# Hybrid encoder layer: earlier attention-to-memory transposes, a held weight load in the MLP loop, and rows added in DRAM at the end

## What is computed

```python
h = rmsnorm(x, g_mix_pre)
q, k, v, u, qx, gates = split(h @ w_in)              # 512, 128, 128, 512, 512, 3 * 1024 columns
y_attn = sliding_window_attention(rope(q), rope(k), v, sinks)
y_ssm  = s5_branch(u, ...)                           # state space, GELU, GLU
y_mem  = memory_cross_attention(qx, km, vm)          # 4 heads, softmax over 256 memory tokens, then @ vm
merged = sum over branches of sigmoid(gate) * (y @ w_branch)
x = x + rmsnorm(merged @ w_out, g_mix_post)          # called x1 below
h = rmsnorm(x, g_mlp_pre)
f = square(relu(h @ w_up)) @ w_down                  # 4096 hidden columns
out = x + rmsnorm(f, g_mlp_post)
```

## Time and profile before

| what | value |
|---|---|
| median of three executions | 1457.79 us |
| the profiled execution, its own time | 1457.39 us |
| its span in the profile | 1455.5 us |
| PE busy | 1438.8 us (99%) |
| DVE busy | 1046.4 us (72%) |
| ACT busy | 524.3 us (36%) |
| POOL busy | 179.6 us (12%) |
| granted TensorE clock | 0.998 of full speed |
| DMA | 209.23 MB, 144 GB/s over the span |

### The profile page before, as it was taken

One profiled execution on the slowest core, in us unless ns is written; L12 is line 12 of the kernel. 1 busy time (PEld: TensorE's weight loads), 2 busy tenths in 40 slices (PEclk: granted clock), 3 DMA queues, 4 the chain that ended last, 5 costly groups with the idle time before them and its releaser, 6 DMA issues. The chain is left out here.

```text
span 1455.5 us, 18397 instructions
## 1 busy us (share of the span) xinstructions
PE 1438.8 (99%) x7046; PEld 1197.9 (82%) x7046; DVE 1046.4 (72%) x1723; ACT 524.3 (36%) x663; POOL 179.6 (12%) x287
## 2 busy tenths in 40 slices
PE   8999999999999999999999999999999999999997
PEld 7888888878888888888898888888888888888885
DVE  6768668647745734446756769697979697979878
ACT  4435853321221352311333532333433343424332
POOL 0000010030000021100100212301110202011110
PEclk9999999999999999999999999999999999999999
DMA  9301121542133187324333446946373727464545
GB/s 333 73 29 58 58 88 58 173 138 93 57 104 119 47 230 290 116 87 160 130 131 87 131 145 204 302 123 209 115 231 105 239 88 220 126 196 143 165 160 188
DMA packets 130322, 209.23 MB, mean 144 GB/s; under 512 B 21480, under 2 KB 72720, under 8 KB 130256
## 3 DMA queue, kind: packets, MB, share of 16 engines
q0 software_dynamic: 46176, 118.26, 25.6%
q1 hardware_dynamic: 84064, 90.07, 18.8%
q10 hardware_dynamic: 16, 0.00, 0.0%
HBM read 168.19 MB, written 40.11 MB: 143 GB/s over the span
## 5 line engine op out<-in xcount | busy, mean ns | idle before, releaser
L2083 PE MATMUL bank<-hThi,whi 128*128 128x512 f32 x800 | 314.0, 392 | 0.1
L2083 PE MATMUL bank<-hThi,wlo 128*128 128x512 f32 x800 | 311.5, 389 | 0.0
L2083 PE MATMUL bank<-hTlo,whi 128*128 128x512 f32 x800 | 311.4, 389 | 0.0
L2083 PEld LDWEIGHTS bank<-hThi,whi 128*128 128x128 f32 x800 | 150.2, 188 | 32.3 <-issue 1.2
L2083 PEld LDWEIGHTS bank<-hThi,wlo 128*128 128x128 f32 x800 | 150.2, 188 | 31.6
L2083 PEld LDWEIGHTS bank<-hTlo,whi 128*128 128x128 f32 x800 | 150.3, 188 | 30.6
L1162 ACT ACTIVATE whi<-raw 128x1024 fp32r<-128x1024 f32 x91 | 95.3, 1055 | 183.4 <-DVE raw L1887 96.8
L1877 DVE TENSOR_TENSOR wlo<-raw,whi 128x1024 fp32r<-128x1024 f32 x91 | 110.9, 1218 | 33.9 <-ACT whi L1162 33.9
L2483 PE MATMUL bank<-hThi,whi 128*128 128x512 f32 x336 | 130.8, 389 | 0.6 <-DMA hTlo<-h_scratch 0.6
L2503 PE MATMUL bank<-whi,yhi 128*128 128x512 f32 x336 | 130.8, 389 | 0.0
L2483 PE MATMUL bank<-hTlo,whi 128*128 128x512 f32 x336 | 130.7, 389 | 0.0
(11 more groups left out here) (398 smaller groups left out, 2563.3 us busy)
## 6 DMA issues: line engine op xcount, KB each, us to landing
hThi<-h_scratch POOLq DMA_DIRECT2D x42, 512.0 KB, 5.6
hTlo<-h_scratch POOLq DMA_DIRECT2D x42, 512.0 KB, 6.5
raw<-in_w_in_dram SPq DMA_DIRECT2D x34, 512.0 KB, 5.4
raw<-in_w_up_dram SPq DMA_DIRECT2D x32, 512.0 KB, 4.4
raw<-in_w_down_dram SPq DMA_DIRECT2D x32, 512.0 KB, 4.5
gate_scratch<-scr POOLq DMA_DIRECT2D x48, 256.0 KB, 2.6
tok<-gate_scratch POOLq DMA_DIRECT2D x24, 512.0 KB, 3.9
yhi<-h_scratch POOLq DMA_DIRECT2D x14, 512.0 KB, 5.8
```

The lines of the kernel that those rows point to most:

```text
L2083: ins = T.matmul(dst, lhs(k)[p], rhs(k)[q], start=start and k == 0 and i == 0, stop=stop and k == kt - 1 and i == 2)
```

## The change

It has three parts.

1. Memory attention: PE's transposes for q = 0 move ahead of the last of the four key/value pieces; ACT's `p_hi_of(0)` moves ahead of `turn(6)` and `turn(7)`; DVE's low parts for q = 0 move ahead of `rope(6)`.
2. The MLP loop: in iteration 0 SP waits for all of S_T3 (`third_in`) before it loads the down-projection weights.
3. The end: `x1` of six of the eight tiles is written straight into `out`, and of two into a smaller `x1_dram`. The inverse roots go to `mx` (DVE, `root`), ACT multiplies six tiles' rows by them in place (128x1024, in `yst` and in `raw`), and POOL adds them to `out` with an accumulating transfer. For the seventh tile ACT scales and POOL itself adds `x1` (`tensor_tensor`), and SP sends it. The eighth tile is finished by DVE as before.

```diff
+ROOTS = [(0, 1), (2, 3), (4, 5), (6,)]
+ROOT_AFTER = {4: 0, 7: 1, 11: 2, 13: 3}
+SCALE_AFTER = {5: (0, 1), 8: (2, 3), 12: (4, 5), 13: (6,)}
...
@@ SP, mlp(m, last)
+                if m == 0:
+                    for landed in third_in:
+                        sp.wait_ge(landed, 32)
                 unit_load(UP0, units[0], w_count(5, m))
                 unit_load(UP1, units[1], w_count(6, m))
...
@@ SP, the end
-            for t in range(NT):
-                sp.wait_ge(out_made, t + 1)
-                if t < NT - 1:
-                    sp.dma_start(rows[tile_of(t)], tok[:, (1 + t % 3) * D:(2 + t % 3) * D]).then_inc(out_sent[t % 3], 16)
...
+            sp.wait_ge(tile_added, 1)
+            sp.dma_start(out_rows[tile_of(NT - 2)], tok[:, 2 * D:3 * D]).then_inc(out_sent, 16)
+            for h in range(2):
+                sp.wait_ge(out_made, h + 1)
+                sp.dma_start(out_rows[tile_of(NT - 1), :, h * 512:h * 512 + 512], tok[:, D + h * 512:D + h * 512 + 512]).then_inc(out_sent, 16)
+            sp.wait_ge(out_sent, 48)
+            for s, count in enumerate((1, 1, 4)):
+                sp.wait_ge(out_added[s], 16 * count)
...
@@ POOL, x1 and the end
-                g.dma_start(x1_dram[t * P:(t + 1) * P, :], yx[:, t % 2, :]).then_inc(x1_sent, 16)
+                g.dma_start(x1_dram[t - tile_of(NT - 2)] if tile_of(t) > 5 else out_rows[t], yx[:, t % 2, :]).then_inc(x1_sent, 16)
...
-            for t in range(3, NT):
-                pool.wait_ge(out_sent[t % 3], 16 * (t // 3))
-                x1_load(t)
+            for t in range(NT - 2):
+                pool.wait_ge(rows_scaled, t + 1)
+                g.dma_start(out_rows[tile_of(t)], last_rows(t), accum_op=add).then_inc(out_added[min(t, 2)], 16)
+            pool.wait_ge(x1_back, 32)
+            pool.wait_ge(rows_scaled, NT - 1)
+            g.tensor_tensor(tok[:, 2 * D:3 * D], last_rows(NT - 2), tok[:, 2 * D:3 * D], add).then_inc(tile_added, 1)
...
@@ ACT, memory attention
-            for k in range(4, 8):
+            for k in range(4, 6):
                 turn(k)
...
             p_hi_of(0)
+            for k in range(6, 8):
+                turn(k)
...
@@ ACT, the end, after the square of piece i
+                for done in SCALE_AFTER.get(i, ()):
+                    k = done // 2
+                    act.wait_ge(root_made, k + 1)
+                    A.activation(last_rows(done), last_rows(done), ACT.Copy, scale=roots(k)[2][:, done % 2:done % 2 + 1]).then_inc(rows_scaled, 1)
...
@@ DVE, memory attention
             for i in range(2, 7):
+                if i == 6:
+                    p_low_of(0)
                 rope(i)
...
@@ DVE, the end
-                for k, t in enumerate(tiles):
-                    xt = tok[:, (1 + t % 3) * D:(2 + t % 3) * D]
-                    dve.wait_ge(x1_back[t % 3], 16 * (t // 3 + 1))
-                    for h in ([slice(0, D)] if t < NT - 1 else [slice(0, 512), slice(512, D)]):
-                        V.scalar_tensor_tensor(out=xt[:, h], in0=yx[:, t % 2, h], scalar=y[:, k:k + 1], in1=xt[:, h], op0=mul, op1=add)\
-                            .then_inc(out_made, 1)
...
+                if t > 5 and s == 0:
+                    dve.wait_ge(out_added[t - 6], 16)
+                mark(V.scalar_tensor_tensor(out=last_rows(t)[:, h], in0=a[:, h], scalar=float(D) ** 0.5, in1=tok[:, h], op0=mul, op1=mul))
+                if i in ROOT_AFTER:
+                    root(ROOTS[ROOT_AFTER[i]], roots(ROOT_AFTER[i]))
+                    dve.sem_inc(root_made, 1)
+            y7 = root((NT - 1,), [stat[:, k:k + 1] for k in range(4)])
+            dve.wait_ge(x1_back, 32)
+            for h in range(2):
+                c = slice(h * 512, h * 512 + 512)
+                V.scalar_tensor_tensor(out=tok[:, D + c.start:D + c.stop], in0=last_rows(NT - 1)[:, c], scalar=y7,
+                                       in1=tok[:, D + c.start:D + c.stop], op0=mul, op1=add).then_inc(out_made, 1)
...
@@ PE, memory attention
-            project(U_KV, FIRST["kv"])
-
+            project(U_KV, FIRST["kv"], range(3))
             pe.wait_ge(x_prob, 16)
...
             x_transposes(0)
+            project(U_KV, FIRST["kv"], range(3, 4))
```

More of the change, by code:

```diff
@@ L291, in hybrid_layer @@
         g_dram = nc.dram_tensor("gate_scratch", (3, KT, P, L), f32, kind="Internal").ap()
-        x1_dram = nc.dram_tensor("x1_scratch", (L, D), f32, kind="Internal").ap()
+        x1_dram = nc.dram_tensor("x1_scratch", (2, P, D), f32, kind="Internal").ap()
         u_dram = nc.dram_tensor("u_scratch", (4, P, L), f32, kind="Internal").ap()
@@ L348, in hybrid_layer @@
         step_made, step_hi, step_lo, step_out = sem("step_made"), sem("step_hi"), sem("step_lo"), [sem(f"step_out{k}") for k in range(2)]
-        x1_back = [sem(f"x1_back{s}") for s in range(3)]
-        out_made, out_sent = sem("out_made"), [sem(f"out_sent{s}") for s in range(3)]
+        root_made, rows_scaled = sem("root_made"), sem("rows_scaled")
+        x1_back, tile_added = sem("x1_back"), sem("tile_added")
+        out_made, out_added, out_sent = sem("out_made"), [sem(f"out_added{s}") for s in range(3)], sem("out_sent")
         chain = sem("chain")
@@ L481, in loaded, with roots, last_rows @@
             return w_loaded[slot], 16 * (2 * ((u - U_QX) // 2 + 1) + 2) + it * 64
+        def roots(k):
+            return [mx[:, 8 * k + 2 * j:8 * k + 2 * j + len(ROOTS[k])] for j in range(4)]
+        def last_rows(t):
+            return yst[:, 2 * (t % 2):2 * (t % 2) + 2, :].rearrange("p a c -> p (a c)") if t < 2 or t > 5 else \
+                raw[:, (t - 2) // 2, (t % 2) * D:(t % 2) * D + D]
+        out_rows = out[0].rearrange("(c i) d -> i c d", i=STEP)
         @block.sync
@@ L1479, in _, with p_low_of @@
             prep_lo(dve, U_KV + 1)
+            def p_low_of(q):
+                for m in range(2):
+                    n = FIRST["xpv"] + pv_event(q, m)
+                    dve.wait_ge(p_high, 2 * q + m + 1)
+                    V.tensor_tensor(p_low(q, m), banks[n % 8][:, :].rearrange("p (t c) -> p t c", t=4),
+                                    pT_hi[:, q % 2, m, :].rearrange("p (t c) -> p t c", t=4).bitcast(f32), sub).then_inc(bank_free[n % 8], 1)
             for i in range(2, 7):
+                if i == 6:
+                    p_low_of(0)
                 rope(i)
@@ L1486, in _ @@
                                   banks[n % 8][:, :].rearrange("p (j c) -> p j c", j=4)).then_inc(bank_free[n % 8], 1)
[L1488 to L1493, removed]
+            for q in range(1, 8):
+                p_low_of(q)
             rope(7)
@@ L2029, in _, with root @@
             up_phase(6, True)
-            def finish(tiles):
+            def root(tiles, places):
                 c, n = slice(tiles[0], tiles[-1] + 1), len(tiles)
-                v, nv, y, w = (stat[:, 2 * k:2 * k + n] for k in (0, 1, 2, 3)) if n == 1 else \
-                    (stat[:, 0:2], stat[:, 2:4], rs[:, 0:2], stat[:, 4:6])
+                v, nv, y, w = places
                 dve.wait_ge(sq_f, LAST_DOWN.index((tiles[-1], 1)) + 1)
@@ L2046, in finish @@
                     do(V.scalar_tensor_tensor(out=y, in0=w, scalar=1.5, in1=y, op0=add, op1=mul))
[L2047 to L2052 removed]
+                return y
             dve.wait_ge(last_gain, 16)
```

23 lines of the change are left out of this document (2 added, 21 removed).

## The result

The changed kernel takes 1460.59 us, the median of 13 runs (1459.08 to 1462.61); the kernel before takes 1457.77 on the same chips (13 runs, 1457.34 to 1458.89). The ratio is 1.0018, with a 95% interval of 1.0010 to 1.0025: 2.8 us slower. The forecast was 1456.9, with a range up to 1459.7, so the result lies outside it.

The account below looks back on a forecast made before the run. PE was taken as the bound, busy 1438.8 of 1455.5 us. Memory attention -1.0, hold +2.6 and end -2.5 summed to -0.9 us, giving a median of 1456.9 us, range 1453.9 to 1459.7.

Parts of the forecast that it names:

- Memory attention, -1.0: Memory attention: PE's 0.97 us wait before the first product with `vm` goes; 1.0 us less, ends 0.8 and 1.2.
- The hold, +2.6: MLP loop, iteration 0: down weights land at 939.6 instead of 936.9, delaying `w_diff` and dP3; 2.6 us more.
- ACT's copy of the first half: MLP loop: ACT's copy moves to about 935.6, its low part done before 938, so it doesn't come last.
- the landing term: MLP loop: the last down weights land at 939.6 in place of 936.9, 2.7 us later.
- The prediction's sign for this part: MLP loop, at dP3: PE would be seen waiting about 3 us for DVE's L1910 of before.
- The end, -2.5: After PE's last matmul: DVE keeps up, its last addition no longer 2.7 us late; less 0.2, 2.5 us less.
- I take no slowing: The end: POOL's addition beside DVE's last product costs DVE nothing; end of the estimate 1.5 us more.
- The rival with its mechanism: The end: POOL's addition blocks DVE, moving its last product and root by 1.0 us; 1457.9 us, chance 0.27.
- the last term: The sum's term for the end: 2.5 us less, or 1.0 by the skill's rule if POOL's addition takes 2.4.
- the 0.2 of the sum: The end: ACT's scalings delay the seventh tile's root and the last square by about 0.2 us, hence 2.7 - 0.2.
- The hold was not free: Rival, MLP loop: down weights still land by 937, dP3 starts as before; -3.6, 1454.2 us, chance 0.2.
- The accumulating transfers were not late: Rival, the end: accumulating transfers at four times a plain one land 3.0 us late; median 1459.9 us, chance 0.1.

Follow-up runs that it names:

- e1: Kernel before with only the memory-attention part (earlier transposes, high and low parts of q = 0): 1457.03 us against 1458.10, ratio 0.9994.
- e4: Changed kernel without the three lines of the hold: 1456.21 us, ratio 0.9983 to the kernel before.
- e3: Kernel before with only the new end: 1456.70 us, ratio 0.9989.
- e8: Kernel before with the hold, and DVE's `left_sum` put ahead of `w_lo_of(7)`: 1462.02 us, ratio 1.0028.
- e7: Kernel before, holding only the second two of the four down-weight transfers until S_T3 has landed: 1459.99 us, ratio 1.0015.
- e2: Kernel before with only the hold of the down-weight loads: 1463.46 us, ratio 1.0035.
- e6: e4 with POOL's addition replaced by a fill, so zeros are sent for the seventh tile: 1455.41 us against 1457.79 before, ratio 0.9982.
- e10: e4 with POOL's addition made to wait for DVE's last product: 1456.66 us, ratio 0.9994 to the kernel before.

## Why the prediction was wrong, step by step

**Memory attention, -1.0: right at its place and in the changed kernel.** -1.2 at the place, -1.07 by e1 (not told from nothing by its interval), and -0.5 as the difference of e4 and e3, where the rest is waited out in uP7. "A shift of PE's list ahead of the end is worth its full size" holds here only because the hold removed that pause.

**The hold, +2.6: wrong, and this decides the sign.** The landing of S_T3, the end of the pause in uP7, SP's issue and the equal shares of the queues came as forecast. That DVE's chain from `w_diff` decides when dP3 starts was right as well. Two steps that say when `w_diff` starts failed.

The first is a term that was put at nothing: "ACT's copy of the first half, released by its landing at 931.4, moves to about 935.6 and is done with its low part before 938, so it doesn't come last." The half landed at 937.74, and its low part was done at 940.1. Its two transfers took as long from issue to landing as before (7.4 and 9.5 us, before 7.5 and 9.9), so that with an issue 6.8 us later the half came 6.3 later, not 4.2. By 938 q1 had moved 1.9 MB, where the half is 1.05 MB, so the four transfers had been under way together. And I asked only whether the low part came before `w_diff`, the wait that I knew, and not what stood behind it in DVE's list. Behind it stood `left_sum`, whose banks PE wanted at 937.7. The two held `w_diff` back by 1.1 us beyond the last landing.

The second is the size of the landing term. It had 2.7 us; the landing was 3.9 later in e8 and, with PE's lead counted in, 4.1 in the changed kernel. The prediction let the first bytes move at about 930, and q1 moved its first in the microsecond from 931. This is why even e8 (4.2) stands above the 2.6, and e7, with two transfers held, near it (2.2). Together 1.4 + 1.1, and 0.1 that the prediction took off because PE would wait less at dP3 (it did not), are the 2.6 us by which the hold's 5.2 was missed.

The prediction's sign for this part, PE waiting about 3 us at dP3, did not show, though the mechanism was there: PE had already stood in uP4 and had only 0.3 us left to wait.

**The clock, not in the sum.** The prediction named no stretch at the lower clock, because PE had no wait over 1.0 us there before. A wait of 4 us brought one, 1.9 us of PE's time in the changed kernel. There it lies under the wait for DVE at dP3; in e2 0.5 us of it reached the end.

**The end, -2.5: mechanism right, size off.** DVE did keep up, and e6 shows the full term, 2.4. With POOL's addition it is 1.15 by the tail and 1.4 by e3. The step was "I take no slowing". The rival with its mechanism, a DVE product held by POOL until it ends, is what happened; its size was 1.4 where the fill's 1.92 us had given 1.0. The Trainium skill ("SBUF — State Buffer", Who interferes with whom) had it: by that rule the last term would be 1.0, and the tail gave 1.15. Its fill that only writes passes, as in e6. The estimate from the Trainium skill's "GPSIMD Engine Reference", Performance versus the Vector engine, was 2.4 us for the addition, and the row says 2.38. I had set the rule aside since no row bore on it; that the row and the rule agreed on the fill was no evidence against it. With ACT's scalings, a pair of 2.18 us, in the way, DVE's last addition starts 0.4 us after PE's end in place of the 0.2 of the sum.

**The rivals.** The hold was not free. The accumulating transfers were not late in the changed kernel: 6.4 us to landing, where a plain one takes 5.6, so nothing like the four times that this rival needed.

With the terms as measured, -1.2 + 5.2 - 1.15 = +2.85, and the medians say 2.8. The hold's error of 2.6 alone would have moved the forecast from 1456.9 to 1459.5; it needed both errors, 2.6 and 1.35, to leave the range.

## What to carry to other kernels

When a load is held back, list every consumer between the landing and the engine that matters, and for each the next operation in that engine's list, whatever it works on: an in-order list turns a late operand of one operation into a late bank of another. Before adding up what an engine lost, find the next place where it meets another: here 4.0 us of standing PE and 1.9 us at half the clock lay beside DVE's list, which was later still, and it was the start of `w_diff` that set the time. An early shift, too, is worth its size only if no wait for a transfer stands behind it. And work that is moved to POOL "for free" was free beside DVE here where POOL only wrote (the fill) or where DVE's operation had one of its two operands in a bank; a POOL operation that reads a single operand was not tried. Splitting POOL's addition or moving it by a few operations only chose which DVE operation paid.

## What the runs showed of the hardware that I had not expected

- A DVE operation with two SBUF operands of one column each, 0.15 us by itself, took 1.21 and 2.15 us beside a POOL addition of 128x512 and 128x1024. It goes both ways: in e10 POOL's addition began while DVE's product ran, and took 2.68 us in place of 2.38. DVE's addition with one operand in a bank (1450.45, 0.68 us) ran beside POOL's at its usual length.
- The granted clock fell after one wait of PE of 4.0 to 4.1 us (0.60 and 0.50 in the four microseconds behind it), and not in e7 or e8, where no wait of its matmuls in the loop was over 1.5 us. The matmuls came 0.43 us apart up to 945.3 in the changed kernel, some 3.5 us, and up to 947.7 in e2, some 4.8.
- An accumulating transfer of 512 KB into DRAM lands 6.4 us after its issue, with little beside it; it is 0.8 above the plain median.
- SP's held transfers were issued from 927.86 on, and the first window of one microsecond in which q1 moves anything is 931 to 932, so some 3 us later, beside POOL's transfers. The queues' share from 933 to 935 us (packets, MB, share of engines) was again equal:

```profile
q1 hardware_dynamic: 201, 0.39, 57.6%
q0 software_dynamic: 187, 0.38, 57.0%
```
